# Two column groups of w_in begun in the first quarter, a third w_o group opened beside the attention lanes, and shorter lane jobs

## The reference, cut to what matters

```python
mod = silu(c) @ w_ada + b_ada                 # 2048 x 12288
shift_a, scale_a, gate_a, shift_f, scale_f, gate_f = split(mod, 6)
h = rms_norm(x, g_attn_pre) * (1 + scale_a) + shift_a
proj = h @ w_in                                # 2048 x 5456
d_q, d_k, d_v, s_q, s_k, s_v, i_q, i_k, i_w = split(proj)
# 8 differential heads: (softmax(q1 k1^T) - lam * softmax(q2 k2^T)) v, then rms_norm
# 8 sparse heads: the indexer scores all keys, the 64 best per query stay, softmax, times v
mixed = concat(diff_out, dsa_out) @ w_o        # 2048 x 2048
x = x + gate_a * rms_norm(mixed, g_attn_post)
# then the feed-forward part, and the second block
```

## Time and profile before

| | us |
|---|---|
| median of three runs | 2319.18 (2318.23 to 2319.81) |
| the profiled execution | 2319.2 |
| its span | 2317.9 |
| TensorE busy in the span | 2253.2 |
| VectorE busy | 1427.4 |
| ScalarE busy | 1081.6 |

### The profile page before, as it was taken

The page is one execution under the profiler, slowest core; times in us unless marked ns, Lnnn a source line. Parts: engine busy times, 40 slices in busy tenths (PEclk is TensorE's granted clock), DMA queues, the critical chain, the costliest instruction groups (busy, mean ns, idle before and its releaser), DMA issues.

```text
span 2317.9 us, 25975 instructions
## 1 busy us (share of the span) xinstructions
PE 2253.2 (97%) x10584; PEld 1842.2 (79%) x10584; DVE 1427.4 (62%) x1940; ACT 1081.6 (47%) x1505; POOL 0.7 (0%) x5
## 2 busy tenths in 40 slices
PE   6999998999999999999999999999999999999998
PEld 3677777878888888888887888888888888888887
DVE  6899787887654677554466545454545555554555
ACT  3435555444444444334445555555344444444443
POOL 0000000000000000000000000000000000000000
PEclk8999999999999999999999999999999999999999
DMA  9987565868555777655554544444555555555553
GB/s 397 398 330 308 201 261 218 316 251 316 200 184 198 263 274 279 219 199 184 198 183 155 208 153 148 163 149 163 205 192 182 200 185 196 184 193 188 190 189 145
DMA packets 79511, 507.70 MB, mean 219 GB/s; under 512 B 8352, under 2 KB 18848, under 8 KB 19744
## 3 DMA queue, kind: packets, MB, share of 16 engines
q1 hardware_dynamic: 79392, 506.05, 59.0%
HBM read 501.82 MB, written 4.19 MB: 218 GB/s over the span
## 4 chain that ended last, share of the span: by engine, by line
PE 88%; DVE 5%; ACT 3%; DMA 2%; issue 1%; SPq 0%; DVEq 0%; ACTq 0%
PE bank L680 28%; PE bank L682 27%; PE bank L681 27%; PE bank L723 1%; PE bank L815 1%; DMA raw<-in_chunks_dram 1%; DVE wlo L1893 1%; DMA P<-in_chunks_dram 1%; ACT whi L1223 1%; PE bank L731 1%; DVE raw L1883 1%; DVE x L1954 0%; DVE raw L1878 0%; PE bank L644 0%; PE bank L838 0%
## 5 line engine op out<-in xcount | busy, mean ns | idle before, releaser
L1893 DVE TENSOR_TENSOR wlo<-raw,whi 128x1024 fp32r<-128x1024 f32 (+2 forms) x744 | 894.8, 1206 | 779.8 <-ACT whi L1223 778.8
L1223 ACT ACTIVATE whi<-raw 128x1024 fp32r<-128x1024 f32 (+2 forms) x744 | 774.5, 1045 | 930.6 <-PE bank L682 900.6
L680 PE MATMUL bank<-whi,Ahi 128*128 128x512 f32 (+2 forms) x2304 | 906.6, 394 | 22.2 <-DVE wlo L1893 14.0
L682 PE MATMUL bank<-whi,Alo 128*128 128x512 f32 (+2 forms) x2304 | 893.3, 388 | 0.0
L681 PE MATMUL bank<-wlo,Ahi 128*128 128x512 f32 (+2 forms) x2304 | 892.9, 388 | 0.0
L680 PEld LDWEIGHTS bank<-whi,Ahi 128*128 128x128 f32 x2304 | 435.0, 189 | 121.9 <-DVE wlo L1893 24.3
L682 PEld LDWEIGHTS bank<-whi,Alo 128*128 128x128 f32 x2304 | 434.8, 189 | 89.4
L681 PEld LDWEIGHTS bank<-wlo,Ahi 128*128 128x128 f32 x2304 | 435.5, 189 | 82.7
L680 PE MATMUL bank<-whi,Fhi 128*128 128x512 f32 x352 | 137.6, 391 | 0.0
L682 PE MATMUL bank<-whi,Flo 128*128 128x512 f32 x352 | 137.0, 389 | 0.0
L681 PE MATMUL bank<-wlo,Fhi 128*128 128x512 f32 x352 | 137.0, 389 | 0.0
(11 more groups left out here) (311 smaller groups left out, 1405.2 us busy)
## 6 DMA issues: line engine op xcount, KB each, us to landing
raw<-in_chunks_dram SPq DMA_DIRECT2D x436, 1024.0 KB, 4.8
P<-in_chunks_dram SPq DMA_DIRECT2D x14, 1024.0 KB, 11.8
G<-in_chunks_dram SPq DMA_DIRECT2D x6, 1024.0 KB, 11.1
raw<-in_chunks_dram SPq DMA_DIRECT2D x8, 768.0 KB, 4.3
raw<-in_chunks_dram SPq DMA_DIRECT2D x8, 576.0 KB, 3.9
x<-in_x_turned_dram SPq DMA_DIRECT2D x2, 1024.0 KB, 12.7
x<-in_x_dram SPq DMA_DIRECT2D x4, 512.0 KB, 7.6
x_spill<-x SPq DMA_DIRECT2D x2, 1024.0 KB, 9.4
```

The costliest lines, as they stand in the source:

```text
L680: pe.matmul(o, a_hi, w_hi, start=beg and kk == 0, stop=False)
L682: ins = pe.matmul(o, a_lo, w_hi, start=False, stop=fin and kk == 1)
L1223: act.activation(m.whi[:, i % NHL, :, 0:n], m.raw_of(c)[:, 2 * h:2 * h + 2, 0:n], ACT.Copy).then_inc(m.s_hi, 1)
L1893: dve.tensor_tensor(m.wlo[:, i % NHL, :, 0:n], m.raw_of(c)[:, 2 * h:2 * h + 2, 0:n], m.whi[:, i % NHL, :, 0:n].bitcast(F32), ALU.subtract) ...
```

## The change

Seven edits, all in the order of work and none in what is computed:

1. Groups 1 and 7 of w_in run over quarter 0 too, behind the five of before (`W_IN_EXTRA`), and later over the three other quarters alone (`left_of`). ScalarE copies their first part, VectorE adds the rest (`add_part`).
2. The scale and shift of quarter 1 are done behind group 2 and group 1 (`SCALE_AFTER`, `SHIFT_AFTER`), those of quarter 2 and 3 behind groups 9 and 0 as before. The tables stay behind group 9 of quarter 0.
3. The w_ada chunks are dealt anew. In quarters 0 to 2, 12, 8 and 4 stand behind w_in chunks, where 11, 7 and 6 stood. In the last quarter three for VectorE stand there, behind groups 9, 0 and 2, where five stood. Five w_in chunks without one lie from the last quarter of group 6 on.
4. `searching` is set from the indexer's last head pair to the end of the search; meanwhile no gate is taken.
5. A third w_o group is opened behind two quarters of groups 0 and 1. Group 0 is set down half done in `y1` and finished later. The second half of the mixed operand is made between the two halves of a chunk (`mid`).
6. Lane a's attention has no empty first step. A differential job does the rope of its queries in its first step and that of its keys in its second, and TensorE's transposes stand in that second step.
7. VectorE, no longer ScalarE, closes groups 1 and 7.

```diff
+W_IN_EXTRA = (1, 7)
+W_IN_PARTS = (W_IN_FIRST + W_IN_EXTRA, W_IN_FIRST, W_IN_FIRST, W_IN_FIRST)
+SCALE_AFTER = ((0, 2), (1, 9), (2, 9))
+SHIFT_AFTER = ((0, 1), (1, 0), (2, 0))
-DEAL_PE = ((3, 3, 2, 2, 1), (2, 2, 1, 1, 1), (2, 2, 2, 0, 0), (0, 0, 0, 0, 0))
+DEAL_PE = ((2, 1, 2, 1, 2, 2, 2), (2, 1, 1, 2, 2), (2, 1, 1, 0, 0), (0, 0, 0, 0, 0))
+DEAL_W_IN = (1,) * 7 + (0,) * 5 + (1,) * 10
@@ can_take
-        return self.taken < len(self.sum_at) and self.unit >= self.sum_at[self.taken] + self.margin
+        return not self.searching and self.taken < len(self.sum_at) and self.unit >= self.sum_at[self.taken] + self.margin
@@ attention, in all three programs
-        if ln is m.lane[1] and k.can_take():
-            ada_take(k.take(), b0)
-        yield
+        if ln is m.lane[1]:
+            if k.can_take():
+                ada_take(k.take(), b0)
+            yield
@@ differential, VectorE
-        for c0 in (C_DQ, C_DK):
-            rope(c0 + 128 * lo, 2 * len(heads), 64, 8, 0, ln, cg, 2 + cg)
-            yield
+        rope(C_DQ + 128 * lo, 2 * len(heads), 64, 8, 0, ln, cg, 2 + cg)
+
+        def turned_keys():
+            rope(C_DK + 128 * lo, 2 * len(heads), 64, 8, 0, ln, cg, 2 + cg)
@@ closing groups 1 and 7, VectorE
+        s = linear("w_in", *win_cols(cg), ks=left_of(cg), before=first_mix if cg == W_IN_ORDER[-1] else None)
+        if cg in W_IN_EXTRA:
+            add_part(s, *win_cols(cg), cg)
@@ w_o, TensorE
-    linear("w_o", 0, 512, m.A_op, mixed, ks=(8,), s=sets[0], begin=False, end=False)
-    need.wait_ge(m.s_dnorm, k.until(("d", 4)))
+    linear("w_o", 0, 512, m.A_op, mixed, ks=(8,), s=sets[0], begin=False)
     linear("w_o", 512, 512, m.A_op, mixed, ks=(8,), s=sets[1], begin=False, end=False)
-    mix_operand(4, (6, 7))
-    linear("w_o", 0, 512, m.A_op, mixed, ks=(4,), s=sets[0], begin=False, end=False)
+    sets.append(k.open())
+    linear("w_o", 1024, 512, m.A_op, mixed, ks=(0,), s=sets[2], end=False)
+
+    def second_mix():
+        need.wait_ge(m.s_dnorm, k.until(("d", 4)))
+        mix_operand(4, (6, 7))
+
+    linear("w_o", 1024, 512, m.A_op, mixed, ks=(8,), s=sets[2], begin=False, end=False, mid=second_mix)
```

More of the change, by code:

```diff
@@ L81, in chunk_plan @@
     assert not first
-    late = len(rest)
-    n = 0
+    deal = iter(DEAL_W_IN + DEAL_W_O)
     def more():
[L87 to L93, removed]
+        for _ in range(next(deal)):
             plan.append(rest.pop(0))
     for cg in W_IN_ORDER:
-        for q in range(4):
-            lin("w_in", 4 * q, *win_cols(cg))
+        for k0 in left_of(cg):
+            lin("w_in", k0, *win_cols(cg))
             more()
[L100 to L107, removed]
+    for k0, g in W_O_PARTS:
+        lin("w_o", k0, 512 * g, 512)
+        more()
     assert not rest
@@ L323, in chunk @@
             self.unit += 1
-            for _ in range(ticks):
-                self.tick()
+            self.tick()
+            if mid and h == 0:
+                mid()
     def last_pass(self, n):
@@ L999, in tensor_program @@
     mix_operand(12, (4, 5))
-    linear("w_o", 512, 512, m.A_op, mixed, ks=(4,), s=sets[1], begin=False, end=False)
-    for g in (0, 1):
+    linear("w_o", 1024, 512, m.A_op, mixed, ks=(4,), s=sets[2], begin=False, end=False)
+    for g in (1, 2):
         linear("w_o", 512 * g, 512, m.A_op, mixed, ks=(12,), s=sets[g], begin=False)
-    linear("w_o", 1024, 512, m.A_op, mixed)
+    linear("w_o", 0, 512, m.A_op, mixed, ks=(4, 12))
     k.last_pass(8)
@@ L1238, in linear @@
                 before(j)
-            k.chunk(w, k0, c0, n)
+            k.chunk(w, k0, c0, n, mid=mid)
         return s
@@ L1369, in q_copies @@
                 copy_out(ln.qT[:, j, :], b, t[j], m.bank[b][:, 0:S])
-        if ln is m.lane[1] and k.can_take():
-            k.take()
-            k.use(b0)
-        yield
+        if ln is m.lane[1]:
+            if k.can_take():
+                k.take()
+                k.use(b0)
+            yield
         t = k.use(b0), k.use(b1)
@@ L2046, in vector_program, with add_part @@
     part_at = {}
+    def add_part(s, c0, n, cg):
+        for tb in range(2):
+            o = m.P1[:, tb, c0:c0 + n]
+            need.wait_ge(m.s_mm, k.unit)
+            released(part_at[cg, tb])
+            dve.tensor_tensor(o, o, m.out_bank(s, tb, n), ALU.add).then_inc(m.freed[2 * s + tb], 1)
     def first_part(q, cg):
@@ L2157, in spread, with attention @@
         return sm[:, 1, :].rearrange("p (t m) -> p t m", t=2).unsqueeze(3).broadcast_to([P, 2, 2, P])
-    def attention(ln, items, scale, nm, v_cg, combine, finish):
+    def attention(ln, items, scale, nm, v_cg, combine, finish, begin=None):
         b0, b1 = ln.bank
         taken = None
-        if ln is m.lane[1] and k.can_take():
-            taken = k.groups[k.take()], b0, k.use(b0)
-        yield
+        if ln is m.lane[1]:
+            if k.can_take():
+                taken = k.groups[k.take()], b0, k.use(b0)
+            yield
         if taken:
@@ L2398, in vector_program @@
         y_at += post_group(m.y1, g, s)
-    s = linear("w_o", 1024, 512)
-    released(mod_at[10])
-    y_at += post_group(m.y1, 2, s)
+    s = linear("w_o", 0, 512, ks=(4, 12))
+    need.wait_ge(m.s_mm, k.unit)
+    for tb in range(2):
+        o = m.y1[:, tb, 0:512]
+        released(part_of_y[tb])
+        dve.tensor_tensor(o, o, m.out_bank(s, tb), ALU.add).then_inc(m.s_part, 1)
+    released(mod_at[8])
+    for tb in range(2):
+        o = m.y1[:, tb, 0:512]
+        need.wait_ge(m.s_psq, k.up(m.s_psq))
+        dve.tensor_tensor(o, o, m.G[:, 0:512], ALU.mult).then_inc(m.freed[2 * s + tb], 1)
+    y_at += set_at(s)
     k.last_pass(8)
```

120 lines of the change are left out of this document (70 added, 50 removed).

## The result

| | us |
|---|---|
| changed kernel, median of 18 runs | 2323.12 (2319.74 to 2325.27) |
| kernel before, beside it, 18 runs | 2318.55 (2316.56 to 2321.95) |
| ratio | 1.0014, 95% interval 1.0008 to 1.0021 |
| profiled execution after | 2320.5, span 2319.2 |
| profiled execution before | 2319.2, span 2317.9 |

The change makes the kernel slower by about 0.14%, 3.2 us by the ratio (the medians differ by 4.6). That is within the 0.2% that I called no change, but 11.5 us above the forecast of 2311.6 and outside the range of 2303 to 2319.

A forecast was written before the change was run, and what follows sets the result against it. Before 472 us, idle time and lowered clock were to gain: loads, then VectorE, then short waits set the pace. -6.7 - 2.0 + 1.4 + 1.0 + 1.5 - 0.8 - 1.0 - 1.0 = -7.6 gave 2311.6 us, range 2303 to 2319.

The forecast's parts named there:

- 1. first quarter: Start of quarter 1: two chunks moved ahead, reached at 90.2 us instead of 96.9, so -6.7; bounds -9.3 to -4.
- 2. indexer's rope: Indexer's rope: two w_ada chunks fewer ahead on VectorE shorten TensorE's wait of 2.3 us to 0.3, -2.0; bounds -2.3 to 0.
- 3. keys' rope, first job: First job's transposes: TensorE waits +1.4 us for the keys' rope if VectorE starts on time, 4.1 if late.
- 3. second job: Second job's first transposes, scores of lane a between: TensorE waits +1.0 us, bounds 0 to 4.
- 4. search: Between the two combines: one gathered wait of 5.1 us, then a lower clock costing 2.6; +1.5, bounds -3 to +2.
- 5. gates elsewhere: Second gate, taken from the idle lane: its wait of 0.8 us goes, -0.8; bounds 0 to -1.1.
- 6. end of group 7: Group 7's end: ScalarE's evacuation no longer stands ahead of exponentials, VectorE's add is hidden; -1.0, bounds 0 to -1.2.
- 7. half 90: Third mixed operand in w_o: wait of 1.9 us stays and grows by about 1.1, two w_ada chunks standing ahead.
- 7. rest of w_o beside the lanes: Run behind half 93 and second operand's wait go, about 5.0 us with drains; new run behind half 98 costs 2.8.
- C: Slower rival, chance 0.10: late VectorE, waits of about 4 us at both ropes and half 98 each costing 2.6 more; 2325.1.

The follow-up runs named there:

- Experiment 1: Changed kernel with the lane steps of before restored in all three programs and both lanes, all else kept: 2313.12 us, ratio 0.9973.
- experiment 5: Kernel of experiment 4, but queries' rope, keys' rope and transposes in three successive steps, a job one step shorter than before: 2310.82 us, ratio 0.9963.
- Experiment 3: Changed kernel with one w_ada chunk behind each w_o chunk, instead of two behind the first and none behind the last: 2318.30 us, ratio 0.9999.
- experiment 9: Kernel before with the third w_o group and the `searching` flag, groups 1 and 7 whole, w_ada deal as before up to w_o: 2319.02 us, ratio 0.9995.
- experiment 6: Kernel before with the new lane steps alone: 2333.12 us, ratio 1.0061.
- experiment 7: First quarter's edits alone, with a deal to fit; lane steps and w_o order of before, no `searching` flag: 2323.05 us, ratio 1.0018.
- experiment 8: Changed kernel with both the lane steps and the w_o order of before, no third w_o group: 2326.20 us, ratio 1.0030.
- experiment 4: Changed kernel with the lane steps of before and one w_ada chunk behind each w_o chunk: 2309.35 us, ratio 0.9957.
- experiment 10: Kernel of experiment 4 with the tables' last part, for lambda, put off from behind group 9 to behind group 0: 2308.34 us, ratio 0.9952.
- experiment 11: Kernel of experiment 4 with the search cut into ten steps instead of six, two rounds between splits: 2310.82 us, ratio 0.9959.
- experiment 2: Changed kernel with VectorE doing the keys' rope in a job's first step behind that of the queries, no step added: 2319.16 us, ratio 1.0001.
- experiment 12: Kernel of experiment 4 with five matmuls whose result nobody reads put ahead of group 2 of quarter 0: 2308.39 us, ratio 0.9951.

## Why the prediction was wrong, by its own steps

What the profiled execution shows, idle time and slow halves against those of before:

| step | predicted | measured |
|---|---|---|
| 1. first quarter | -6.7 | -7.7 |
| last quarter, its first eight halves | none | -1.1 |
| 2. indexer's rope | -2.0 | -0.9 |
| 3. keys' rope, first job | +1.4 | +5.7 |
| 3. second job | +1.0 | 0 |
| a sparse head's result, at 307.69 us | none | +1.4 |
| 4. search | +1.5 | +1.1 |
| 5. gates elsewhere | -0.8 | -0.8 |
| 6. end of group 7 | -1.0 | -0.6 |
| 7. half 90 | +1.1 | +4.6 |
| 7. rest of w_o beside the lanes | -2.1 | -1.7 |
| low parts at 456 and 468 us | none | +1.2 |

The measured column sums to +1.2, and the span grew by 1.3. That they agree so closely is partly luck: single entries are good to some tenths. The two largest misses are at the keys' rope and at half 90, and both have the same two parts: a wait longer than forecast, and a slow half behind it that the sum had at nothing.

**Keys' rope, 4.3 us too low.** The step assumed "if VectorE starts on time", and step 2 counted two chunks of w_ada fewer in the last quarter, 4.8 us of VectorE. It didn't start on time. TensorE passed the step at 176.89 and VectorE began its add at 179.59, 2.70 us late, exactly as late as before:

```profile
179.59 1.28 DVE L2075 TENSOR_TENSOR P<-P,bank 128x512 f32<-128x512 f32 x2
...
184.47 1.28 DVE L1905 CUSTOM_DVE_ANT_0 raw<-raw,csb,modT 128x1024 f32<-128x1024 f32 x1
...
187.94 0.28 DVE L2160 TENSOR_TENSOR P<-rt 128x128 f32<-128x128 f32 x1
```

Its absolute time hardly moved either (178.82 before). VectorE was busy for 14.93 of the 15 us from 166 on, in the changed kernel (above) and in the one before, whose window is this:

```profile
166.00:181.00 15.00, 12.48 (x58) 9.10 (x57) 14.93 (x31) 5.47 (x8) 0.00 (x0) 1.00 0.20 70
```

What became of the relief the rows at the half behind it show, first before, then after, TensorE's half and VectorE's add of group 8:

```profile
155.77 0.41 PE L680 MATMUL bank<-whi,Ahi 128*128 128x512 f32 x1
157.89 1.28 DVE L2057 TENSOR_TENSOR P<-P,bank 128x512 f32<-128x512 f32 x2
```

```profile
158.45 0.39 PE L681 MATMUL bank<-whi,Ahi 128*128 128x512 f32 x1
158.65 1.28 DVE L2075 TENSOR_TENSOR P<-P,bank 128x512 f32<-128x512 f32 x2 [0.40 <-PE bank L683]
```

VectorE was 2.1 us behind TensorE there before and 0.2 after: it had caught up and stood idle for a part of the time (0.44, 1.40 and 0.40 us between 152 and 159). From that add to that of group 2 its work is the same in both kernels, 20.9 us. TensorE, with shorter waits, passed the same stretch in 18.4 us (158.45 to 176.89) instead of 20.4 (155.77 to 176.12), and so was 2.70 us ahead again. The chunks were taken from where VectorE could catch up, and the three that stayed stand where it is the bound. The prediction had counted on all of the 4.8 us of relief; 1.9 of them arrived, TensorE's own shorter waits used them up, and none was left for the keys' rope. The bound that I gave for this case, 4.1, is the wait that came, 4.06. What I left out even there is the slow half behind it (1.67), though the prediction's own had shown one behind 3.86. Experiment 1 gives the price of the whole edit, 10.0 us in the medians, and experiment 5 the cause: rope and reader in one step. Of the second job the forecast was wrong too, though its number looks right: TensorE never waits for its keys' rope. The 1.43 us at 307.69 are for a sparse head's result, and stand in experiment 1 as well (1.67), with the old steps.

**Half 90, 3.5 us too low.** The size was off twice: 4.11 instead of 3.0, and again the clock, 2.4 us. VectorE's reductions of the two chunks stood ahead of the operand, as the prediction said:

```profile
362.18 1.28 DVE L1900 CUSTOM_DVE_ANT_0 raw<-raw,csb,bT 128x1024 f32<-128x1024 f32 x1
...
363.51 1.28 DVE L1905 CUSTOM_DVE_ANT_0 raw<-raw,csb,modT 128x1024 f32<-128x1024 f32 x1
...
367.11 1.28 DVE L1951 TENSOR_TENSOR Alo<-bank,Ahi 128x512 fp32r<-128x512 f32 x2
```

Experiment 3 takes 2.45 us of wait and the slow half away by one table entry, 4.8 us in the medians.

**Two low parts, 1.2 us, not foreseen.** At 455.95 and 467.66 (halves 114 and 118) TensorE waits 0.63 and 0.53 us for VectorE, which is busy 60.58 us in 412 to 479, before 56.01. They have two causes. At half 114 VectorE has just finished group 0 of w_o, which edit 5 had set down half done; experiment 9, with that order and the 13 chunks of w_ada beside w_o that were there before, waits there too (0.83), and experiments 6, 7 and 8, with the order of before, don't. At half 118 it is the deal, 16 chunks where 13 were: the wait stands in experiments 7 and 8 (0.69 and 0.67 us, with 15 and 16 chunks), and not in 9.

What was right: the first quarter in every place (group 8 at 43.19, forecast 43.9; the wait at the tables 4.47, forecast 4.7; quarter 1 at 89.16, forecast 90.2), and the search. But the reason for the search was half wrong: the changed kernel's program is the same with the `searching` flag and without it, because the new deal leaves no gate to be taken there. Where the flag acts, in experiment 9, the search loses 2.6 us. The one rival that ended slower, C, had the right mechanism (long waits, gathered, each with a slow half) at one of its three places and at one it didn't name, so that its 2325.1 comes within 2 us of the median is in part luck.

One thing the sum of single edits could not show, though it cost this forecast nothing: the first quarter has no worth without the third w_o group. It gives about 9 us under the new w_o order (experiment 9 against 4), and with the old one the lead turns into a loss (experiments 7 and 8), because the halves that it takes from beside the lanes were their cover.

Open is the 2.6 us between the profiled execution and the median of the changed kernel. Halves behind the same wait took different times from trace to trace: 4.23, 4.43 and 5.28 us at the tables, 4.52 and 4.90 behind the keys' rope. With four such places that could make 2 us or more; this is an estimate from those differences, not shown for this kernel's median. One such place before the lanes is enough: the traces of the changed kernel and of experiment 1, whose programs are the same up to there, are 2.1 us apart at quarter 1 (89.16 and 91.24), and half of that is the half at the tables. Nor is it confined to the changed stretch: at 1231 us, in the second block, the clock falls behind the same two short waits (0.79 and 1.67 us) in the traces of before and after, and not in those of experiments 1 and 4.

## What to carry to other kernels

When an engine is brought forward, ask of each later meeting whether the other engine was brought forward too; a lead is worth nothing until every handover has room for it. Relief for an engine is worth something only where that engine is the bound; given earlier, it is idled away. Give a producer one step between its result and the reader: the one step saved there cost some 8 us, where all else together won 10. Price edits that shift work past a bound stage together, and test them in pairs.

## What the runs showed of the hardware

A wait lowers TensorE's clock for the work behind it, but its length alone doesn't decide whether, nor for how long. I had taken the point to lie between the 2.3 us of the kernel before, which had left the clock alone, and the 3.86 that had not. In experiment 6 a wait of 2.29 us, at the very place of those 2.3, was followed by a half of 4.19 us (178.04 less 173.85):

```profile
173.18 0.55 PE L731 MATMUL bank<-const,P 128*128 128x128 f32 x2 [2.29 <-DVE P L2134]
...
173.85 0.78 PE L680 MATMUL bank<-whi,Ahi 128*128 128x512 f32 x1
...
178.04 0.38 PE L731 MATMUL bank<-const,P 128*128 128x128 f32 x2
```

In experiment 10, behind the wait of 2.95 us, the first matmuls ran at full speed and the next seven took 0.63 us, at half the clock:

```profile
66.17:69.16 2.99, 2.99 (x9) 2.30 (x8) 2.08 (x5) 1.78 (x3) 0.00 (x0) 0.50 1.01 425
```

The trace of before holds such a case that I had passed over: behind the gate's wait of 2.72 us, at 256.16, the clock is 0.50 from 257 to 259. In experiment 11 waits of 1.42 and 0.37 us close together were enough: seven matmuls of 0.63 us followed. The wait of 1.84 in experiment 2 left the clock alone, and so did one of 2.38 us at 45.37 in experiment 9. Behind one and the same wait of 2.87 us ahead of half 120, all twelve matmuls of the half are slow in the trace of before, seven in experiment 1 and none in experiment 7. Filled with matmuls that nobody reads, a wait of the length that otherwise dropped the clock left it at 1.00 (experiment 12). The Trainium skill, "Perfetto Trace Analysis", Matmul Optimizations, says that the engine scales its power with utilization; by that rule, the trace agrees.
